# Mixing stage of a hybrid decoder layer: memory attention moved beside the last projections, block attention interleaved with the second inversion

## The reference

```python
qkv = jax.nn.silu(causal_depthwise_conv(...))          # A: gated DeltaNet, 4 heads x 128, chunks
a_mat = jnp.where(strict, (k_beta @ k.T) * decay, 0.0)
u = triangular_solve(a_mat + I, v * beta)              # inverse of a unit triangular matrix
w = triangular_solve(a_mat + I, k_beta * exp(gc))
v_new = u_i - w_i @ state                              # scan over the chunks
o_i = (q_i * exp(g_i)) @ state + a_i @ v_new
state = state * exp(g_last) + (k_i * ...).T @ v_new
# B: MoBA block attention, 4 heads x 64, causal with ALiBi and QK-norm
# C: memory attention, 4 heads x 64, 256 memory tokens
p = softmax(qh @ kh.T * Dh ** -0.5); out = p @ vh
x = x + concat(A, B, C) @ W_out
```

## Time and profile before

| | us |
|---|---|
| median of 3 runs | 1105.69 (1102.08 to 1107.39) |
| the profiled execution's own time | 1103.15 |
| its span | 1101.4 |
| PE busy | 1066.9 (97%) |
| DVE busy | 554.7 (50%) |
| POOL busy | 388.2 (35%) |
| ACT busy | 370.0 (34%) |
| mean granted TensorE clock | 0.978 |

### The profile page before, as it was taken

One profiled execution on the slowest core, in us unless ns is written; L12 is line 12 of the kernel. 1 busy time (PEld: TensorE's weight loads), 2 busy tenths in 40 slices (PEclk: granted clock), 3 DMA queues, 4 the chain that ended last, 5 costly groups with the idle time before them and its releaser, 6 DMA issues.

```text
span 1101.4 us, 14682 instructions
## 1 busy us (share of the span) xinstructions
PE 1066.9 (97%) x5840; PEld 879.2 (80%) x5840; DVE 554.7 (50%) x844; ACT 370.0 (34%) x520; POOL 388.2 (35%) x109
## 2 busy tenths in 40 slices
PE   9999999999999999999987788999999999999998
PEld 7988888888888788789775567888888888888886
DVE  5864434445344679923335763383544343454444
ACT  7522222232222434243354554152222222222210
POOL 0354444343435314332421101063534353534340
PEclk9999999999999999999996988999999999999999
DMA  8342232323232312322010000131332323232311
GB/s 298 118 151 88 103 114 76 114 76 114 76 114 76 115 39 77 115 77 77 31 49 1 2 1 1 39 115 61 131 109 82 114 76 114 78 113 76 114 38 76
DMA packets 15735, 94.71 MB, mean 86 GB/s; under 512 B 2128, under 2 KB 2128, under 8 KB 5456
## 3 DMA queue, kind: packets, MB, share of 16 engines
q1 hardware_dynamic: 15696, 94.17, 24.0%
HBM read 92.06 MB, written 2.10 MB: 85 GB/s over the span
## 4 chain that ended last, share of the span: by engine, by line
PE 92%; DVE 3%; ACT 3%; issue 1%; DMA 1%; SPq 0%; POOL 0%; DVEq 0%; ACTq 0%
PE bank L1194 83%; ACT prob L621 1%; PE bank L1517 1%; PE bank L1427 1%; DMA x<-x_in 1%; PE bank L1214 1%; PE bank L1520 1%; PE bank L1462 1%; DVE xn L1031 1%; PE bank L1707 0%; ACT prob L624 0%; PE bank L1685 0%; PE bank L1581 0%; DVE rowmax L1047 0%; DVE prob L1045 0%
## 5 line engine op out<-in xcount | busy, mean ns | idle before, releaser
L379 POOL TENSOR_TENSOR wlo<-raw,whi 128x2048 fp32r<-128x2048 f32 x80 | 370.1, 4628 | 617.5 <-ACT whi L438 604.2
L1194 PE MATMUL bank<-ahi,whi 128*128 128x512 f32 x944 | 370.6, 393 | 0.5 <-DVE alo L740 0.5
L1194 PE MATMUL bank<-ahi,wlo 128*128 128x512 f32 x944 | 368.6, 391 | 0.0
L1194 PE MATMUL bank<-alo,whi 128*128 128x512 f32 x944 | 368.6, 390 | 0.0
L438 ACT ACTIVATE whi<-raw 128x2048 fp32r<-128x2048 f32 x80 | 152.7, 1911 | 348.8 <-PE bank L1194 326.3
L1194 PEld LDWEIGHTS bank<-ahi,whi 128*128 128x128 f32 x944 | 178.1, 189 | 38.4 <-ACT ahi L460 0.9
L1194 PEld LDWEIGHTS bank<-ahi,wlo 128*128 128x128 f32 x944 | 178.0, 189 | 37.3
L1194 PEld LDWEIGHTS bank<-alo,whi 128*128 128x128 f32 x944 | 178.1, 189 | 36.5
L861 DVE SCALAR_TENSOR_TENSOR x<-bank,x 128x512 f32<-128x512 f32 x176 | 121.4, 690 | 89.9 <-PE bank L1194 89.2
L1194 PE MATMUL bank<-hhi,whi 128*128 128x512 f32 x352 | 137.2, 390 | 1.8 <-DVE x L861 1.7
L1194 PE MATMUL bank<-hlo,whi 128*128 128x512 f32 x352 | 137.0, 389 | 0.0
(11 more groups left out here) (251 smaller groups left out, 859.2 us busy)
## 6 DMA issues: line engine op xcount, KB each, us to landing
raw<-stream SPq DMA_DIRECT2D x80, 1024.0 KB, 4.8
raw<-stream SPq DMA_DIRECT2D x6, 512.0 KB, 5.8
x<-x_in SPq DMA_DIRECT2D x4, 512.0 KB, 7.6
out<-x SPq DMA_DIRECT2D x8, 256.0 KB, 2.0
raw<-stream SPq DMA_DIRECT2D x4, 256.0 KB, 6.9
memx<-mem_in SPq DMA_DIRECT2D x2, 512.0 KB, 10.5
cst<-const_in SPq DMA_DIRECT2D x1, 480.0 KB, 5.8
cst<-const_in SPq DMA_DIRECT2D x1, 256.0 KB, 5.6
```

The costliest lines, as they stand in the source:

```text
L379: nc.gpsimd.tensor_tensor(wlo[:, u % RING, :], raw[:, u % RAW, :], whi[:, u % RING, :].bitcast(F32), ALU.subtract).then_inc(w_lo, 1)
L1194: ins = E.matmul(dst, a, b, start=(n == 0 and i == 0), stop=(n == last and i == 2))
```

## The change

The arithmetic is the same; the order on PE, DVE, ACT and POOL, the banks and the buffers are new.

- The cq projection comes before mq and mk, and the mv tiles come last. Each of tiles 14 and 16 to 21 is issued in two halves of 12 matmuls (`in_part`), with small work between the halves.
- Memory attention runs in eight pairs of heads (`mem_scores`, `mem_turn`, `mem_out`) between those half tiles and the levels of the first inversion, with buffers and banks of its own. Its result waits in `cq` and is split into high and low parts later (`mem_result`, `mem_low_part`).
- A level of the inversion treats both chunks of its pair in one pass: one mask instruction instead of two, two or three ACT copies for both, two DVE subtractions for both. The first half of the level writes to one transposition bank and two product banks.
- Block attention also runs in pairs of heads (`scores`, `turn`, `values`): scores and turn of each pair stand in the levels of the second inversion, together with chunks 0 and 1 of the scan, which is no longer held back until that inversion ends. Chunks 2 and 3 of the scan follow it.
- The decay factors of chunk 3 get a buffer of their own. The SiLU of z moves from before the block attention to after the scan, and the two key-norm spreads move into levels 4 and 5 of the first inversion.

The core of the diff, on PE (the lists on DVE, ACT and POOL are rewritten to match):

```diff
@@ masks on POOL, one for both chunks
-                for j in range(2):
-                    nc.gpsimd.tensor_tensor(bm[pair][:, j, :, :], at_[:, j, :, 0:DH], over_heads(level(l)),
-                                            ALU.mult).then_inc(b_ready, 1)
+                mask = level(l).unsqueeze(1).broadcast_to([P, 2 * H, DH])
+                nc.gpsimd.tensor_tensor(bm[pair][:].rearrange("p j h t -> p (j h) t"),
+                                        at_[:, :, :, 0:DH].rearrange("p j h t -> p (j h) t"), mask,
+                                        ALU.mult).then_inc(b_ready, 1)
@@ a projection tile in parts
+            def in_part(q, n, a, k0, k1):
+                if k0 == 0 and q >= 4:
+                    pe.wait_ge(p_evac, q - 3 if q < 14 else q - 1)
+                for k in range(k0, k1):
+                    i = split_product(psum[in_bank(q)][:], wparts(U_IN + n, k, a * P, P, 256), ...)
@@ the order on PE, first inversion, one level
-            for l in range(1, LEVELS):
-                level_first(0, l)
-                if l <= 4:
-                    in_tile(21 + l, n, (l - 1) % 2)
-                level_second(0, l)
+            in_part(20, 10, 0, 0, K2)
+            mem_turn(1)
+            level_first(0, 2)
+            in_part(20, 10, 0, K2, KD)
+            mem_out(1)
+            mem_scores(3)
+            level_second(0, 2)
...
+            level_second(0, 5)
+            prep_decay(2)
+            mem_turn(5)
+            level_first(0, 6)
+            prep_decay(3)
+            mem_out(5)
+            mem_scores(7)
+            level_second(0, 6)
+            mem_turn(6)
+            prep(2)
+            mem_out(6)
+            scores(0)
+            prep(3)
+            mem_turn(7)
+            prep_turn(2)
+            mem_out(7)
+            prep_turn(3)
+            scores(1)
+            level_zero(1)
@@ the order on PE, second inversion, one level
-                level_first(1, l)
-                attention(A_LEVEL + 2 * (l - 1))
-                level_second(1, l)
-                attention(A_LEVEL + 2 * (l - 1) + 1)
+            level_first(1, 3)
+            turn(2)
+            scan_v(1)
+            level_second(1, 3)
+            values(2)
+            scores(4)
+            scan_s(1)
...
+            scores(7)
+            scan_v(2)
+            turn(6)
+            scan_s(2)
+            values(6)
+            scan_k(3)
+            scan_o(2)
+            turn(7)
+            scan_v(3)
+            values(7)
+            scan_o(3)
```

More of the change, by code:

```diff
@@ L643, in _ @@
+            square(1)
+            act.wait_ge(g_dve, 4)
+            A.activation(gate(G_EG, 3), gate(G_GC, 3), ACT.Exp).then_inc(g_act, 1)
+            weight_hi(U_IN + 9)
+            square(2)
+            sqrt(5, 16, 32)
+            square(3)
+            weight_hi(U_IN + 10)
             act.wait_ge(gates_ready, 1)
             prep_decay(0)
+            square(4)
+            mem_weights(0)
+            prep_keys(0)
+            prep_values(0)
+            prep_decay(1)
+            square(5)
@@ new lines, in _ @@
+            prep_decay(3)
+            mem_weights(7)
+            mem_copy(6)
+            weights(0)
+            prep_keys(2)
+            prep_values(2)
+            mem_copy(7)
+            prep_keys(3)
+            prep_values(3)
+            level_copy(1, 1)
+            copy(0)
+            weights(1)
+            scan_v(0)
+            result(0)
+            level_copy(1, 2)
+            copy(1)
+            weights(2)
+            scan_o(0)
+            result(1)
+            level_copy(1, 3)
@@ L656, in _ @@
+            copy(6)
+            result(6)
+            scan_o(2)
+            scan_v(3)
+            copy(7)
+            result(7)
+            scan_o(3)
             for t in range(H):
[L657 removed]
+                act.wait_ge(p_evac, 18 + t + 1)
                 A.activation(z[:, t, :], z[:, t, :], ACT.Silu).then_inc(z_ready, 1)
[L659 to L663 removed]
@@ L1174, in _ @@
             x_low(2, S_G2, KD - 1)
[L1176 removed]
+            x_stat(2, 8)
             ffn(1)
@@ L1514, in level_first @@
+                x = xn[pair]
+                if l < LAST:
+                    pe.wait_ge(b_ready, n_b(pair, l) + 1)
+                    for j in range(2):
                         for q in range(2):
@@ new lines, in _ @@
+            level_first(1, 1)
+            turn(0)
+            scan_v(0)
+            level_second(1, 1)
+            values(0)
+            scores(2)
+            scan_s(0)
+            level_first(1, 2)
+            turn(1)
+            scan_o(0)
+            level_second(1, 2)
+            values(1)
+            scores(3)
+            scan_k(1)
+            level_first(1, 3)
+            turn(2)
+            scan_v(1)
+            level_second(1, 3)
+            values(2)
+            scores(4)
@@ new lines, in _ @@
+            scan_s(1)
+            level_first(1, 4)
+            turn(3)
+            scan_o(1)
+            level_second(1, 4)
+            values(3)
+            scores(5)
+            scan_k(2)
+            level_first(1, 5)
+            turn(4)
+            level_second(1, 5)
+            values(4)
+            scores(6)
+            level_first(1, 6)
+            turn(5)
+            level_second(1, 6)
+            values(5)
+            scores(7)
+            scan_v(2)
+            turn(6)
```

1144 lines of the change are left out of this document (661 added, 483 removed).

## The result

The changed kernel takes 1078.42 us (median of 4 runs, 1076.83 to 1078.99) against 1105.35 for the kernel before on the same chip: ratio 0.9757, 95% interval 0.9731 to 0.9783. A second set, beside experiments 5 to 7, gave 1079.68 us (6 runs, 1078.66 to 1080.29), ratio 0.9791, interval 0.9759 to 0.9823; 1078.4 within 2 us was expected of it. The forecast was 1088 in a range of 1076 to 1101. The direction, the mechanism and the range held; the number was 9.6 us too high, and lies next to the 1077 of rival one.

What follows compares the result with a forecast made beforehand. PE's own order of events bounds the kernel (97% busy). Tile 12 to output norm: 185.1 us at full clock plus 13.9 for the clock, 199 against 215.0; from 1103.15 gives 1087.1, plus 1 for runs: 1088, range 1076 to 1101.

Steps and rivals of the forecast that it cites:

- rival one: The clock stays up in C to E: 1077 us; chance 0.20.
- A: Start of tile 12 to level 1 of the first inversion: 59.0 us at full clock, 63.3 before.
- B: First inversion's level 1 to second half of level 5, with memory attention: 48.0 us at full clock, 36.1 before.
- D: Second inversion, level 1 to end of level 6, with half the scan: 34.6 us at full clock, 31.7 before.
- E: Rest of scan and attention, up to the output norm's statistics: 22.0 us at full clock, 55.5 before.
- The walk at full clock: Engine orders followed from tile 12 to the output norm: 185.1 us at full clock, against 215.0 before.
- C: First inversion's level 5 to level 1 of the second, preparing chunks 2 and 3: 21.5 us, 28.4 before.
- memory copy 7: In C, this copy queues on ACT behind `prep_keys(2)` and `prep_values(2)`, leaving 2.3 us open.
- the clock's term: Charge for half clock: 3.4 us in A, 3.0 in C, 5.0 in D, 2.5 in E, together 13.9.
- Two: Block attention's ring paces the second inversion's six levels, each paying one more 2 us wait: 1100 us; chance 0.15.
- Three: The clock falls in C and stays at 1.2 GHz until the output norm (L1707): 1114 us; chance 0.05.
- The SiLU: On ACT before the output norm's square root: about 3.5 us with table load, fits idle time, costed at nothing.

Runs made afterwards that it cites:

- experiments 5 to 7: Kernel after with query/key norm's end later on DVE (1072.62 us); with four ACT/PE places changed (1070.1); with those four, POOL's split and `scan_r(1)` moved (1065.08).
- experiment 3: Kernel after with all eight memory attention pairs moved behind the first inversion, one behind another: 1102.74 us, ratio 0.9987 to before.
- experiment 2: Kernel after with all scan chunks behind the last level of the second inversion: 1085.13 us, ratio 0.9841 to before.
- experiment 8: Kernel before with nine extra constant products filling two of PE's waits between the inversions: 1097.65 us against 1105.18, ratio 0.9937.
- experiment 5: Kernel after with the end of the query and key norm moved on DVE behind `level_zero(0)` and `mem_max(1)`: 1072.62 us, ratio 0.9726 to before.
- experiment 1: Kernel after with projection tiles 19, 20 and 21 not cut in halves: 1083.39 us, ratio 0.9818 to before.

## Why the prediction was right, and where not

**The mechanism.** Memory attention bought with PE time in A and B and taken off the round trips of D and E: shown by experiment 3, which alone loses 23 to 24 us, by the order and by the clock that it keeps. Half of the scan in the levels: shown by experiment 2, 5.4 to 6.7 us.

**The walk at full clock.** From two profiles of the kernel after and the experiments, 3.4 us at half clock cost 1.5 in A (58.6 against 57.1 us from the transposition of the gates, L1610, to level 1), 1.6 in B's first level (10.8 against 9.2), 1.3 in D's (6.5 against 5.2) and 1.6 in E (30.4 against 28.8 from level 5 to the statistics). The second profile's fall in C cost 1.0 (23.7 against 22.7). Taken off, after has

| stretch | before | before, filled | predicted at full clock | after | after, second profile | after less its clock |
|---|---|---|---|---|---|---|
| A | 63.3 | 61.8 | 59.0 | 64.2 | 62.6 | 62.7 |
| B | 36.1 | 36.2 | 48.0 | 46.9 | 46.9 | 45.3 |
| C | 28.4 | 25.3 | 21.5 | 22.7 | 23.7 | 22.7 |
| D | 31.7 | 28.7 | 34.6 | 35.6 | 34.4 | 34.3 |
| E | 55.5 | 53.2 | 22.0 | 20.5 | 20.5 | 18.9 |
| sum | 215.0 | 205.1 | 185.1 | 189.9 | 188.0 | 183.9 |

The walk's 185.1 against 183.9 is good partly by luck: A lacked the 3.0 us of the held norm, B was 2.7 too long and E 3.1. In E the walk had laid the parts of three engines end to end; ACT's and DVE's parts overlapped PE's more. B is PE's work throughout, so its prices a level or pair were a little high; which of them was not tried apart. Why C came out 1.2 above its sum was not tried. The periods that the prediction gives for D add up to 34.8, not 34.6, which changes nothing. Of the waits named, `prep_turn(0)` (1.3, it is 1.31), memory copy 7 (2.3, it is 2.32) and level 3's `rsb` (1.5, it is 1.47) came as put.

**The step that failed: the clock's term.** "C is 70% busy on PE in my walk (before, 71%), so it will fall there again: 3.0 in C, 5.0 in the first two levels of D, 2.5 in E", with 3.4 in A: 13.9. Measured: 1.5, 1.6, 0, 1.3 and 1.6 in A to E, together 6.0; in the second profile 0, 1.6, 1.0, 0 and 1.6, together 4.2. In C PE was busy for 16.9 of 22.7 us (74%) and the clock stayed at 1.00 until its last 0.2 us; its longest wait was 2.32 us, where before it was 3.95. But in the second profile the same C lost 1.0 us: there the clock did fall, at 596.64, 0.9 us after PE's wait for memory copy 7 had ended, stayed at half for 3.4 us and was back before level 1. So the prediction had the place of a fall about right and its length wrong: no profile of after has the long stay at half that the earlier trace rows show, and what was charged as 3.0 and 5.0 us in C and D is one fall of 1.0 to 1.3 us in one or the other. What decides the length is open; the busy share of the stretch does not tell it, since experiment 3 stayed at 0.50 with PE busier. In A one of the two falls charged came, in the second profile none.

By the first profile the charge was 7.9 of the 9.1 us by which the 199 missed 189.9; the other 1.2 is the walk. With the 6.0 in its place the number would have been 1080. The Trainium skill (TensorE: Matmul & The Clock Gate, Part 1: The HAM clock gate) calls the slow clock the default that activity releases; that by itself does not say why it stayed at 0.50 through PE at 81% busy in experiment 3, and what the rule wants of PE is not shown by any run here.

**How much was the clock.** Before to after, A to E lost 25.1 us. Filling (experiment 8) took 9.9 us off the kernel before with 34.1 us of half clock; 6.8 us of it remained, some 3 us more by the prices above, which puts its full-clock sum near 202. After is at 183.9. So about 18 us of the gain is order at equal clock and 7 the clock. The split is an estimate: the filled kernel's extra products may hide or cost tenths, and each side is one profile.

**What was not seen coming.** The wait of 2.96 us ahead of level 1. The prediction weighed DVE's queue by durations from before, where these operations did not stand beside a split. The Trainium skill (SBUF — State Buffer, Who interferes with whom) says that a DVE instruction with two SBUF inputs contends with a GpSimd instruction that reads SBUF, and that of two that contend the one issued second is blocked until the first has ended. This trace agrees: L812, begun 0.12 us after the split, ended 0.04 us after it, L810 in experiment 5 0.05 us after it, and L810 in after, begun 0.08 us ahead of a mask, took 0.19; while L1119 (one input in PSUM) and the reciprocal (one input), both beside POOL's work in experiment 5, took their usual 0.69 and 0.34. Two inputs are not the whole of it: a scaling of a tile in SBUF (L1163, usually 0.35) was held as well, in experiment 1 beside a split that ran from 546.62 to 551.20:

```profile
547.31 4.04 DVE L1163 TENSOR_SCALAR mem_prob<-mem_prob,rowinv 128x256 f32<-128x256 f32 x1
```

The prediction didn't use any of this, though it bore on this change, which put new work on POOL's and DVE's orders side by side, and though its own trace had the 4.94 us of L916.

**Rivals.** One came out in its number and half in its reason: the clock was at half for 6.8 us of C to E in both profiles, once each in D and E or once each in C and E, where before it was 34.1. Two did not come: no level of D is over 7.4 us, and DVE waits for no exponentials. Three did not come, but experiment 3 shows it can: 34 us on end at 1.2 GHz. The SiLU cost nothing: PE has no wait from the statistics on to 700 us. That ACT is idle for 3.82 us ahead of the square root, as for 3.79 before, does not show it by itself: what ended it is DVE's mean, and DVE was held there too (L1309, 4.41 us beside a split that ended at 667.02):

```profile
667.50 0.22 ACT L450 ACTIVATE stat_root<-stat_mean 128x16 f32<-128x16 f32 x1 [3.82 <-DVE stat_mean L801]
```

## What to carry to other kernels

Put work that makes round trips where the matmul engine is already the bound, and check its cover by halves of a tile, not by the share of a stretch. When an order is laid out by hand for four engines, place GpSimd's long operations against the VectorE operations that have two SBUF inputs or scale a tile in SBUF: a 0.2 us operation can become 4.5 us, and it shows as busy time, not as a wait. A wait of a few us ahead of matmuls costs more than its length where the clock falls behind it: here 3.0 us of wait and 1.6 us for the fall behind it, and the kernels without the wait were 7 to 9 us shorter in all. So small waits on the chain are worth clearing even at 98% busy. Where the clock is part of the sum, take two profiles of the same kernel before a fall is given to a place.

## What the runs showed of the hardware that was not expected

- DVE held inside an instruction by POOL: 4.47 us for a 128x32 operation beside a 4.55 us split, 0.19 without it; 1.18 beside a mask of 1.28; and 4.04 instead of 0.35 for a scaling with one tensor input (experiment 1).
- Work added to PE made the kernel before 7.5 us faster (ratio 0.9937, interval 0.9923 to 0.995).
- PE at 81% busy for 16 us with the granted clock at 0.50 throughout (experiment 3), and at 74% over 22.7 us with 1.00 (C of the kernel after, first profile; 0.93 in the second).
- A profile of the same kernel differs from another in where its clock falls: A to the first level was 58.6 us with 3.4 us at half and 57.1 with none, and the part from the statistics to the end 419.6 us with 6.8 at half and 421.2 with 10.2. Comparisons of single profiles carry 1.0 to 1.6 us for each such fall.
